# Blocked triangular solves on one NeuronCore: doubling-step products on half of the moving columns

## The chip, the core and the metric

The kernel runs on one core of a Trainium2 chip. TensorE multiplies a stationary operand (loaded into its array by a weight load) with a moving operand that streams through it, and writes to PSUM. VectorE (DVE) and ScalarE (ACT) do the elementwise work and copy results out of PSUM, SyncE (SP) issues the weight transfers from HBM, and GpSimd (POOL) does a little set-up. The engines run side by side and wait for each other with semaphores. The metric is the time of one execution on the device in microseconds (us). The median of three runs of the kernel before is 2916.0 us (2914.81 to 2918.55).

## What is computed

Two networks run one after the other on 256 tokens of width 1024: first two layers with feed-forward blocks and a four-way mixer (convolution, RWKV-7, retention, latent attention), then a pooling layer, a gated delta rule layer ("deltanet") and a mixture of experts. The change touches the two places where a recurrence is computed by chunks of 64 tokens. There a unit lower triangular 64x64 system is solved for each head and chunk:

```
a = jnp.einsum('bhnid,bhnjd->bhnij', k_beta, k) * decay
a = jnp.where(strict, a, 0.0) + jnp.eye(c, dtype=a.dtype)
u = lax.linalg.triangular_solve(a, v_beta, left_side=True, lower=True, unit_diagonal=True)
w = lax.linalg.triangular_solve(a, k_beta * jnp.exp(gc)[..., None],
                                left_side=True, lower=True, unit_diagonal=True)
```

In the reference the RWKV mixer is a scan over tokens, forward and backward. The kernel computes it by chunks too, so it has the same kind of system: a lower triangular one for the forward direction and an upper triangular one for the backward direction.

## The kernel before

Each engine has one program, written out by hand in a fixed order. Parts follow each other (`LAYER_PLAN` twice in a hardware loop, then `SECOND_PLAN`). Weights stream in 1 MB tiles through a ring of six buffers, `raw`; ScalarE rounds each tile to its high part (L282), VectorE makes the low part (L285), and TensorE multiplies with both. The RWKV part and the delta rule part (`rk_tensor`, `dn_core_tensor`) need few or no weights; their time is that of a long chain between TensorE and VectorE.

A triangular matrix is inverted by doubling. `T` holds the inverse of the diagonal blocks of a size, `TT` its transpose, `LT` the transpose of the off-diagonal matrix with its sign. The first doubling (blocks of 1 to 2) is made by VectorE before the solve. Five levels (`LEVELS`, `lv` 0 to 4) do the rest, blocks of 2, 4, 8, 16, 32:

- Y = L·T, then masked by VectorE to the off-diagonal block of each pair of blocks (L1131 on TensorE, L1151 on VectorE)
- T is increased by T·Y (L1140, added at L1157); the last level leaves this out
- TT is increased by the transpose of that product (L1144, added at L1161)

A solve has 16 matrices for each `d` (0 and 1), stacked as 8 groups of 64 columns by two halves of the 128 partitions (`HALVES`: partitions 0 to 63 and 64 to 127). So each product of a level is a group of 16 matmuls, 64 stationary columns by 64 moving columns, and the profile shows two records for an fp32 matmul: 32 records a group. The two halves use different rows and columns of the array. The names `rk_T`, `rk_TT`, `rk_Y`, `rk_LT` lie in the tensors `U` and `work`; those of the delta rule lie in `work`. `d` is the direction in the RWKV part and the token tile in the delta rule part. There are three solves: one in each of the two layers' RWKV part, and one in the delta rule.

Order of one level: TensorE does Y of d=0 and d=1, then an `extra` (at level 0 the RWKV part multiplies `rk_MK` by `rk_V`, L1328; at levels 0 to 3 the delta rule part transposes eight 128x128 tiles, L2037), then for each d T's product and TT's product. VectorE does the two masks, then T's and TT's sum for each d. TensorE waits for the mask of a `d` before T's product, and for T's sum before the next Y. After the RWKV solve TensorE goes on with L1406, and VectorE does L1564, the low part of a weight tile (L285) and the copies L1572, for which L1414 waits. After the delta rule's solve TensorE goes on with L2076.

Of the kernel before, what the change touches and what calls it, by code (L numbers as in the profile page):

```python
# [22 lines left out]
ALU = mybir.AluOpType  # L23
# [7 lines left out]
TT = S // P  # L31
# [143 lines left out]
def build(nc, a, out):  # L175

    with ExitStack() as ctx:
# [63 lines left out]
        f = {k: sem(k) for k in FLAGS + SOLVE_FLAGS}  # L241
# [868 lines left out]
        Y_BANK, ZT_BANK, ZTT_BANK = (0, 3), (1, 4), (2, 5)  # L1110
# [5 lines left out]
        def bank(i):  # L1116
            return ps[:, i, :].rearrange("p (g m) -> p g m", m=64)

        def eighths(r, i, g):
            return ps[r, i, g * 64:(g + 1) * 64]  # L1120

        def solve_tensor(pe, LT, T, TT, Y, first, extra):

            for lv in range(LEVELS):
                for d in range(2):
                    pe.wait_ge(f[f"sol_T{d}"], lv + 1)
                    if lv == 0:
                        first(d)
                    for g in range(8):
                        for r in HALVES:  # L1130
                            mm = pe.matmul(eighths(r, Y_BANK[d], g), LT[d][r, g, :], T[d][r, g, :], start=True, stop=True)  # L1131
                    mm.then_inc(f[f"sol_y{d}"], 1)
                extra(lv)
                for d in range(2):
                    pe.wait_ge(f[f"sol_ysb{d}"], lv + 1)
                    pe.wait_ge(f[f"sol_TT{d}"], lv + 1)
                    if lv < LEVELS - 1:
                        for g in range(8):
                            for r in HALVES:
                                mm = pe.matmul(eighths(r, ZT_BANK[d], g), TT[d][r, g, :], Y[d][r, g, :], start=True, stop=True)  # L1140
                        mm.then_inc(f[f"sol_z{d}"], 1)
                    for g in range(8):
                        for r in HALVES:
                            mm = pe.matmul(eighths(r, ZTT_BANK[d], g), Y[d][r, g, :], TT[d][r, g, :], start=True, stop=True)  # L1144
                    mm.then_inc(f[f"sol_z{d}"], 1)

        def solve_vector(dve, T, TT, Y, masks):
            for lv in range(LEVELS):
                for d in range(2):
                    dve.wait_ge(f[f"sol_y{d}"], lv + 1)  # L1150
                    dve.tensor_tensor(Y[d], bank(Y_BANK[d]), mask64(masks[d], lv + 1), ALU.mult) \  # L1151
                       .then_inc(f[f"sol_ysb{d}"], 1)
                dve.drain()
                for d in range(2):
                    if lv < LEVELS - 1:
                        dve.wait_ge(f[f"sol_z{d}"], 2 * lv + 1)
                        dve.tensor_tensor(T[d], T[d], bank(ZT_BANK[d]), ALU.add).then_inc(f[f"sol_T{d}"], 1)  # L1157
                        dve.wait_ge(f[f"sol_z{d}"], 2 * lv + 2)
                    else:
                        dve.wait_ge(f[f"sol_z{d}"], 2 * lv + 1)  # L1160
                    dve.tensor_tensor(TT[d], TT[d], bank(ZTT_BANK[d]), ALU.add).then_inc(f[f"sol_TT{d}"], 1)  # L1161
                dve.drain()

        CH = 64
# [31 lines left out]
        rk_B, rk_MK, rk_RK, rk_Kt, rk_T, rk_TT, rk_LT, rk_Y = ([carve_one() for _ in range(2)] for _ in range(8))  # L1196
# [14 lines left out]
        MASKS = (("low64", "up64", "strict_up64", "incl_up64"), ("up64", "low64", "strict_low64", "incl_low64"))  # L1211
# [120 lines left out]
        def eights(pair):  # L1332
            return [by_eight(v) for v in pair]
# [41 lines left out]
        def rk_tensor(pe, n, l):  # L1375
            pe.wait_ge(f["rk_kx"], 1)
            for b in range(2):
                mm = pe.matmul(half_of(2, b), const("bdones"), by_pair(rk_ksum)[:, b, :], start=True, stop=True)
# [11 lines left out]
            for b, c in BLOCKS:  # L1390
                for r in HALVES:
                    mm = pe.matmul(ps[r, 0, slot(b, c)], U[r, U_V + b, c * 64:(c + 1) * 64], eye64[r, :],
                                   start=True, stop=True)
# [2 lines left out]
            mix_out_tensor(pe, n, 2)  # L1396
            for d in range(2):
                rk_build_tensor(pe, d)
            solve_tensor(pe, eights(rk_LT), eights(rk_T), eights(rk_TT), eights(rk_Y), lambda d: rk_first_tensor(pe, d),
                         lambda lv: rk_x_tensor(pe) if lv == 0 else None)  # L1400
            for d in range(2):
                pe.wait_ge(f[f"sol_TT{d}"], LEVELS + 1)
# [139 lines left out]
        def rk_vector(dve, n, l):  # L1542
# [16 lines left out]
            for d in range(2):  # L1559
                refill_vector(dve, n + d + 1)  # L1560
                rk_evacuate_vector(dve, d)
            solve_vector(dve, eights(rk_T), eights(rk_TT), eights(rk_Y), (MASKS[0][0], MASKS[1][0]))
            for b in range(2):
                st = dve.scalar_tensor_tensor(out=by_pair(rk_prod)[:, b, :], in0=U[:, U_R + b, :],  # L1564
                                              scalar=layer_vec("rwkv_r_k")(b), in1=by_pair(rk_ksum)[:, b, :],
# [475 lines left out]
        def dn_core_tensor(pe):  # L2041
# [25 lines left out]
                if lv < 4:  # L2067
                    dn_turn_tensor(pe, 2 + lv, *((DN_V, 1), (DN_K, 1), (DN_Q, 0), (DN_Q, 1))[lv])

            solve_tensor(pe, dn_LT, dn_T, dn_TT, dn_Y, first, extra)  # L2070
            pe.wait_ge(f["dn_taken"], 6)
            for t in range(TT):
                pe.wait_ge(f[f"sol_TT{t}"], LEVELS + 1)
# [131 lines left out]
        def dn_core_vector(dve):  # L2205
# [16 lines left out]
            d_()  # L2222
            for t in range(TT):
                dve.tensor_tensor(dn_TT[t], dn_TT[t], bc(const("stack"), NH), ALU.add).then_inc(f[f"sol_TT{t}"], 1)
            solve_vector(dve, dn_T, dn_TT, dn_Y, ("low64", "low64"))
            for t in range(TT):
                dve.wait_ge(f["dn_u"], t + 1)
                dve.tensor_copy(dn_U[:, t], wide_two(2 + 2 * t)).then_inc(f["dn_us"], 1)
# [733 lines left out]
```

## Time and profile before

| | |
|---|---|
| median of three runs | 2916.0 us |
| profiled execution, its own time | 2916.18 us |
| its span | 2914.4 us |
| TensorE busy, share of the span | 93% |
| VectorE busy | 66% |
| ScalarE busy | 49% |
| mean granted TensorE clock | 0.969 of 2.4 GHz |
| first RWKV solve | 377.90 to 407.30 us |
| second RWKV solve | 1012.60 to 1042.10 us |
| delta rule solve | 1685.20 to 1720.10 us |

A busy share is an average over stages with different limits. The three solves take about 94 us of the 2914.4, so they are read by themselves: in the timeline, row by row, which engine starts as soon as which other has ended. A row of the timeline merges equal instructions: its start, its length from the first's start to the last's end, the engine, the line, the operation, and in brackets how long the engine sat idle before it and who released it. A matmul record's own length (219 ns here) is longer than the distance from one to the next, since they overlap; the rate is read from starts.

### The profile page before, as it was taken

The page shows a single profiled execution, that of the slowest core. Times are in us where ns is not written, and L with a number is a line of the kernel's source. Part 1 is how long each engine was busy: PE and PEld are TensorE (multiplying, and loading weights), DVE is VectorE, ACT ScalarE, POOL GpSimd, SP SyncE. Part 2 cuts the span into 40 slices and gives each one's busy share as a digit, 9 for nine tenths or more (in the row PEclk, how much of TensorE's full clock was granted, in tenths as well). Part 3 has the DMA queues.
Part 4 walks back from the last instruction along what each step waited for, and adds up shares of the span by engine and source line. Part 5 has one row for each costly group of instructions (what it writes and reads, how often), then busy time and mean ns, then how long its engine had stood idle before and what let it go on. Part 6 is the DMA issues. An engine that isn't in the chain of part 4 may idle for free.

```text
span 2914.4 us, 49969 instructions
## 1 busy us (share of the span) xinstructions
PE 2703.1 (93%) x20144; PEld 2382.9 (82%) x20144; DVE 1911.3 (66%) x1750; ACT 1419.3 (49%) x1330; POOL 84.6 (3%) x82
## 2 busy tenths in 40 slices
PE   8999989999999989986999896899999989999997
PEld 8988888989998879976999795687777777777876
DVE  4555765555555854555556645688878878888886
ACT  4343513343343513342336532566757666666665
POOL 6000005000000000000000000000000000000000
PEclk9999999999999999997999998899999999999999
DMA  7553213545553205542555400799989989999995
GB/s 274 181 191 130 93 46 130 187 159 174 187 189 107 94 17 184 187 156 87 187 187 146 145 3 8 283 338 344 344 292 340 342 296 336 337 342 336 341 346 197
DMA packets 340994, 602.08 MB, mean 207 GB/s; under 512 B 11968, under 2 KB 178752, under 8 KB 340672
## 3 DMA queue, kind: packets, MB, share of 16 engines
q1 hardware_dynamic: 333184, 590.84, 59.2%
q10 hardware_dynamic: 7616, 8.58, 0.9%
q8 instruction: 130, 2.13, 0.3%
q14 instruction: 64, 0.52, 0.1%
HBM read 598.34 MB, written 1.05 MB: 206 GB/s over the span
## 4 chain that ended last, share of the span: by engine, by line
DMA 54%; PE 22%; DVE 12%; ACT 8%; DVEq 2%; issue 1%; SPq 1%; another core or an unknown queue 0%; ACTq 0%; PEldq 0%; PEld 0%; POOLq 0%
DMA raw<-in_moe_w_up 26%; DMA raw<-in_ffn_w_down 22%; DVE wlo L285 8%; ACT whi L282 6%; PE ps L781 5%; PE ps L665 3%; DMA raw<-in_w_in 2%; PE ps L419 2%; PE ps L434 1%; PE ps L381 1%; DMA raw<-in_dn_w_out 1%; DMA raw<-in_dn_w_in 1%; DMA raw<-in_pool_w_in 1%; PE ps L1144 1%; PE ps L1131 1%
## 5 line engine op out<-in xcount | busy, mean ns | idle before, releaser
L285 DVE TENSOR_TENSOR wlo<-raw,whi 128x2048 fp32r<-128x2048 f32 x562 | 1286.4, 2289 | 623.1 <-ACT whi L282 621.7
L282 ACT CAST whi<-raw 128x2048 fp32r<-128x2048 f32 x562 | 1071.5, 1907 | 686.0 <-DMA raw<-in_ffn_w_down 171.5
L419 PE MATMUL ps<-xhi,whi 128*128 128x256 f32 x1760 | 500.4, 284 | 2.5 <-DVE xlo L369 2.5
L419 PE MATMUL ps<-xlo,whi 128*128 128x256 f32 x1760 | 498.7, 283 | 0.0
L419 PE MATMUL ps<-xhi,wlo 128*128 128x256 f32 x1760 | 498.7, 283 | 0.0
L2474 PE MATMUL ps<-whi,xhi 128*128 128x512 f32 x896 | 367.6, 410 | 21.3 <-remote 20.1
L2474 PE MATMUL ps<-whi,xlo 128*128 128x512 f32 x896 | 352.6, 394 | 0.0
L2474 PE MATMUL ps<-wlo,xhi 128*128 128x512 f32 x896 | 352.3, 393 | 0.0
L419 PEld LDWEIGHTS ps<-xhi,whi 128*128 128x128 f32 x1760 | 338.0, 192 | 5.2 <-DVE xlo L369 2.7
L419 PEld LDWEIGHTS ps<-xhi,wlo 128*128 128x128 f32 x1760 | 338.0, 192 | 1.9
L419 PEld LDWEIGHTS ps<-xlo,whi 128*128 128x128 f32 x1760 | 338.0, 192 | 0.0
L2474 PEld LDWEIGHTS ps<-whi,xhi 128*128 128x128 f32 x896 | 170.2, 190 | 62.2 <-issue 29.4
L2474 PEld LDWEIGHTS ps<-whi,xlo 128*128 128x128 f32 x896 | 169.8, 190 | 37.4
L2474 PEld LDWEIGHTS ps<-wlo,xhi 128*128 128x128 f32 x896 | 170.4, 190 | 36.2 <-issue 3.8
L2499 PE MATMUL ps<-whi,hhi 128*128 128x512 f32 x448 | 181.6, 405 | 15.5 <-DVE wlo L285 12.9
L434 PE MATMUL ps<-whi,hhi 128*128 128x512 f32 x472 | 185.7, 394 | 10.5 <-remote 7.2
L434 PE MATMUL ps<-wlo,hhi 128*128 128x512 f32 x472 | 184.5, 391 | 0.0
L434 PE MATMUL ps<-whi,hlo 128*128 128x512 f32 x472 | 183.9, 390 | 0.0
L2499 PE MATMUL ps<-whi,hlo 128*128 128x512 f32 x448 | 175.8, 392 | 0.0
L2499 PE MATMUL ps<-wlo,hhi 128*128 128x512 f32 x448 | 175.5, 392 | 0.0
L2499 PEld LDWEIGHTS ps<-whi,hhi 128*128 128x128 f32 x448 | 84.5, 189 | 54.6 <-issue 37.7
L487 ACT ACTIVATE work<-ps 128x512 f32<-128x512 f32 x55 | 32.9, 598 | 193.2 <-PE ps L419 193.2
(498 smaller groups left out, 3780.3 us busy)
## 6 DMA issues: line engine op xcount, KB each, us to landing
raw<-in_moe_w_gate SPq DMA_DIRECT2D x112, 1024.0 KB, 5.1
raw<-in_moe_w_up SPq DMA_DIRECT2D x112, 1024.0 KB, 5.1
raw<-in_moe_w_down SPq DMA_DIRECT2D x112, 1024.0 KB, 4.9
raw<-in_ffn_w_gate SPq DMA_DIRECT2D x55, 1024.0 KB, 5.0
raw<-in_ffn_w_up SPq DMA_DIRECT2D x55, 1024.0 KB, 5.0
raw<-in_ffn_w_down SPq DMA_DIRECT2D x55, 1024.0 KB, 4.8
raw<-in_w_in SPq DMA_DIRECT2D x26, 1024.0 KB, 5.0
raw<-in_dn_w_in SPq DMA_DIRECT2D x16, 1024.0 KB, 5.6
```

Source lines behind the costliest of these rows:

```text
L282: act.copy(whi[:, n % SPLIT, 0:width], raw[:, n % RAW, 0:width]).then_inc(hi_ready[n % SPLIT], 1)
L285: dve.tensor_tensor(wlo[:, n % SPLIT, 0:width], raw[:, n % RAW, 0:width], whi[:, n % SPLIT, 0:width], ALU.subtract).then_inc(split_ready[n ...
L381: mm = pe.matmul(turned_x(c, first)[:, t * P:(t + 1) * P], x[:, t, c * P:(c + 1) * P], turn[:, t, :], start=True, stop=True)
L419: mm = pe.matmul(dst[:, b * ntok:(b + 1) * ntok], w[:, n % SPLIT, c * GW + b * P:c * GW + (b + 1) * P], xt[part][:, c, 0:ntok], start=(c = ...
L434: mm = pe.matmul(ps[:, banks[2 * t + s], :], hp[part][b][:, t * P:(t + 1) * P], w[:, n % SPLIT, b * D + s * HALF:b * D + (s + 1) * HALF], ...
L487: act.activation(sil[:, q, 0:w], ps[:, 4 + q, 0:w], ACT.Silu)
L665: mm = pe.matmul(ps[0:m, bank, 0:S], wv, xt[:, c, :], start=first, stop=last)
L781: mm = pe.matmul(half_of(bank_, b, slice(0, m)), wv, xt[:, c, :], start=first, stop=last)
L1131: mm = pe.matmul(eighths(r, Y_BANK[d], g), LT[d][r, g, :], T[d][r, g, :], start=True, stop=True)
L1144: mm = pe.matmul(eighths(r, ZTT_BANK[d], g), Y[d][r, g, :], TT[d][r, g, :], start=True, stop=True)
L2474: mm = pe.matmul(dst, (xhi, xlo)[part][:, k * C // 2 + c, xhalf(q)], w[:, (m + k) % SPLIT, c * EW:(c + 1) * EW], start=(k == 0 and c == 0 ...
L2499: mm = pe.matmul(ps[:, s, :], (hh, hl)[part][:, g % 2, 2 * k + b, :], w[:, (m + k) % SPLIT, b * D + s * HALF:b * D + (s + 1) * HALF], star ...
```

## The change

The step of a level fills only half of the columns of T, and half of those of TT. For a lower triangular system these are, in T, the columns of the first block of each pair of blocks, and in TT those of the second; for an upper triangular one the other way round (`upper`, 0 or 1 for each d). The change multiplies and adds only these. Two helpers take the columns: at level `lv` the runs are `m = 2 << lv` columns long, every second run is taken, so 16 runs of 2 columns at level 0, 8 of 4, 4 of 8, 2 of 16, and at level 4 one run of 32.

The moving operand of all three products goes from 64 to 32 columns, and so does the output region in PSUM. The stationary operand stays 64 columns wide, the number of matmuls is the same, and so are all waits. The sums L1157 and L1161 go from 512 to 256 elements a partition. The mask L1151 still works on all 512 elements of Y, of which half are now what an earlier product left in that PSUM bank; the mask sets these to zero.

```diff
+        def half_cols(v, lv, other):
+
+            return v.rearrange("p (k a m) -> p k a m", a=2, m=2 << lv)[:, :, other, :]
+
+        def half_groups(v, lv, other):
+            return v.rearrange("p g (k a m) -> p (g k) a m", a=2, m=2 << lv)[:, :, other, :]
...
-                            mm = pe.matmul(eighths(r, Y_BANK[d], g), LT[d][r, g, :], T[d][r, g, :], start=True, stop=True)
+                            mm = pe.matmul(half_cols(eighths(r, Y_BANK[d], g), lv, upper[d]), LT[d][r, g, :],
+                                           half_cols(T[d][r, g, :], lv, upper[d]), start=True, stop=True)
...
-                                mm = pe.matmul(eighths(r, ZT_BANK[d], g), TT[d][r, g, :], Y[d][r, g, :], start=True, stop=True)
+                                mm = pe.matmul(half_cols(eighths(r, ZT_BANK[d], g), lv, upper[d]), TT[d][r, g, :],
+                                               half_cols(Y[d][r, g, :], lv, upper[d]), start=True, stop=True)
...
-                            mm = pe.matmul(eighths(r, ZTT_BANK[d], g), Y[d][r, g, :], TT[d][r, g, :], start=True, stop=True)
+                            mm = pe.matmul(half_cols(eighths(r, ZTT_BANK[d], g), lv, 1 - upper[d]), Y[d][r, g, :],
+                                           half_cols(TT[d][r, g, :], lv, 1 - upper[d]), start=True, stop=True)
...
-                        dve.tensor_tensor(T[d], T[d], bank(ZT_BANK[d]), ALU.add).then_inc(f[f"sol_T{d}"], 1)
+                        part = half_groups(T[d], lv, upper[d])
+                        dve.tensor_tensor(part, part, half_groups(bank(ZT_BANK[d]), lv, upper[d]), ALU.add) \
+                           .then_inc(f[f"sol_T{d}"], 1)
...
-                    dve.tensor_tensor(TT[d], TT[d], bank(ZTT_BANK[d]), ALU.add).then_inc(f[f"sol_TT{d}"], 1)
+                    part = half_groups(TT[d], lv, 1 - upper[d])
+                    dve.tensor_tensor(part, part, half_groups(bank(ZTT_BANK[d]), lv, 1 - upper[d]), ALU.add) \
+                       .then_inc(f[f"sol_TT{d}"], 1)
```

The instructions themselves show it. On TensorE, from the last matmuls of the build to level 1 of the RWKV solve, before (xN counts the matmuls of the program, two records each; the last figures are partitions x moving columns):

```order
L1313 MATMUL ps<-work 64x128 x16
L1131 MATMUL ps<-U 64x64 x32
L1328 MATMUL ps<-U,work 64x64 x32
L1140 MATMUL ps<-U 64x64 x16
L1144 MATMUL ps<-U 64x64 x16
L1140 MATMUL ps<-U 64x64 x16
L1144 MATMUL ps<-U 64x64 x16
L1131 MATMUL ps<-U 64x64 x32
L1140 MATMUL ps<-U 64x64 x16
```

and after, where lines are renumbered (L1138, L1148, L1153 are the three products, L1342 the extra):

```order
L1327 MATMUL ps<-work 64x128 x16
L1138 MATMUL ps<-U 64x16x2 x32
L1342 MATMUL ps<-U,work 64x64 x32
L1148 MATMUL ps<-U 64x16x2 x16
L1153 MATMUL ps<-U 64x16x2 x16
L1148 MATMUL ps<-U 64x16x2 x16
L1153 MATMUL ps<-U 64x16x2 x16
L1138 MATMUL ps<-U 64x8x4 x32
L1148 MATMUL ps<-U 64x8x4 x16
```

Nothing moved; the moving operand is 16 runs of 2 columns in place of 64 columns at level 0, and 8 runs of 4 at level 1.

On VectorE, from the sums of level 3 to the copies that stand behind the RWKV solve, before:

```order
L1157 TENSOR_TENSOR U<-U,ps 128x512
L1161 TENSOR_TENSOR U<-U,ps 128x512
L1151 TENSOR_TENSOR U<-ps,con 128x512 x2
L1161 TENSOR_TENSOR U<-U,ps 128x512 x2
L1564 SCALAR_TENSOR_TENSOR U<-U,cur 128x256 x2
L252 ISA
L285 TENSOR_TENSOR wlo<-raw,whi 128x2048
L1572 COPY work<-ps 128x256
```

and after (L1161 is now the mask, L1168 and L1174 are the sums, L1586 the copy):

```order
L1168 TENSOR_TENSOR U<-U,ps 128x16x16
L1174 TENSOR_TENSOR U<-U,ps 128x16x16
L1161 TENSOR_TENSOR U<-ps,con 128x512 x2
L1174 TENSOR_TENSOR U<-U,ps 128x8x32 x2
L1578 SCALAR_TENSOR_TENSOR U<-U,cur 128x256 x2
L252 ISA
L285 TENSOR_TENSOR wlo<-raw,whi 128x2048
L1586 COPY work<-ps 128x256
```

Again the order is the same. The sums have half the elements, the masks all of them.

## Rows read from the trace of the kernel before

**Rows 1.** Page, part 4: the chain that ended last, by line

```profile
DMA raw<-in_moe_w_up 26%; DMA raw<-in_ffn_w_down 22%; DVE wlo L285 8%; ACT whi L282 6%; PE ps L781 5%; PE ps L665 3%; DMA raw<-in_w_in 2%; PE ps L419 2%; PE ps L434 1%; PE ps L381 1%; DMA raw<-in_dn_w_out 1%; DMA raw<-in_dn_w_in 1%; DMA raw<-in_pool_w_in 1%; PE ps L1144 1%; PE ps L1131 1%
```

**Rows 2.** Stretches: us, busy (x records) of the engines, PEclk, DMA share, GB/s

```profile
377.90:407.30 29.40, 28.50 (x964) 28.40 (x960) 20.25 (x30) 1.21 (x3) 0.00 (x0) 1.00 0.08 27
...
1690.00:1693.00 3.00, 3.00 (x39) 2.67 (x39) 0.00 (x0) 1.60 (x7) 0.00 (x0) 0.50 0.00 0
...
1732.40:1736.00 3.60, 3.60 (x69) 3.60 (x65) 0.69 (x1) 1.01 (x1) 0.00 (x0) 1.00 0.02 5
```

**Rows 3.** Timeline, level 1 of the first RWKV solve: start, length, engine, line

```profile
386.45 2.06 PE L1131 MATMUL ps<-U 64*64 64x64 f32 x64
...
387.62 0.69 DVE L1151 TENSOR_TENSOR U<-ps,con 128x512 f32<-128x512 f32 x1 [0.24 <-PE ps L1131]
...
388.36 1.15 PE L1140 MATMUL ps<-U 64*64 64x64 f32 x32
...
389.35 1.10 PE L1144 MATMUL ps<-U 64*64 64x64 f32 x32
...
390.28 1.10 PE L1140 MATMUL ps<-U 64*64 64x64 f32 x32
...
391.21 1.10 PE L1144 MATMUL ps<-U 64*64 64x64 f32 x32
...
392.14 2.03 PE L1131 MATMUL ps<-U 64*64 64x64 f32 x64
```

**Rows 4.** Timeline, end of the first RWKV solve and what follows

```profile
403.50 2.03 PE L1131 MATMUL ps<-U 64*64 64x64 f32 x64
...
407.33 3.71 PE L1406 MATMUL ps<-work,U 64*64 64x128 f32 x64
407.52 0.69 DVE L1161 TENSOR_TENSOR U<-U,ps 128x512 f32<-128x512 f32 x1 [0.25 <-PE ps L1144]
408.31 0.88 DVE L1564 SCALAR_TENSOR_TENSOR U<-U,cur 128x256 f32<-128x256 f32 x2
409.11 2.28 DVE L285 TENSOR_TENSOR wlo<-raw,whi 128x2048 fp32r<-128x2048 f32 x1
...
411.53 0.42 DVE L1572 COPY work<-ps 128x256 f32<-128x256 f32 x1
...
412.34 0.33 PE L1414 MATMUL ps<-U,work 64*64 64x64 f32 x4 [1.30 <-DVE U L1572]
```

**Rows 5.** Timeline, end of the delta rule's solve

```profile
1719.33 0.69 DVE L1161 TENSOR_TENSOR work<-work,ps 128x512 f32<-128x512 f32 x1 [0.31 <-PE ps L1144]
1720.13 1.75 PEld L2076 LDWEIGHTS ps<-work 64*64 64x64 f32 x32
```

**Rows 6.** Groups by shape, VectorE: a sum with PSUM of 256 elements

```profile
L992 DVE TENSOR_TENSOR U<-ps,rope 32x256 f32<-32x256 f32 x2 | 0.8, 422 | 0.2
```

**Rows 7.** Timeline, weight loads of 128 columns for one moving column

```profile
1575.35 0.98 PEld L1847 LDWEIGHTS ps<-con,work 128*128 128x128 f32 x8
...
1576.25 0.19 PEld L665 LDWEIGHTS ps<-xhi,whi 128*128 128x128 f32 x1
```

**Rows 8.** Timeline, 128 stationary columns: 128 moving columns, then 64

```profile
1727.62 0.27 PE L2096 MATMUL ps<-U,work 64*128 64x128 f32 x1
...
1729.07 0.27 PE L2096 MATMUL ps<-U,work 64*128 64x128 f32 x1
...
1733.77 0.27 PE L2115 MATMUL ps<-rope,U 64*128 64x64 f32 x1
...
1735.78 0.27 PE L2117 MATMUL ps<-con,U 64*128 64x64 f32 x1
```

**Rows 9.** Timeline, delta rule's solve, level 0: two groups of 32 records

```profile
1691.30 1.98 PE L1140 MATMUL ps<-work 64*64 64x64 f32 x32
...
1693.06 1.17 PE L1144 MATMUL ps<-work 64*64 64x64 f32 x32
```

More of the change, by code:

```diff
@@ L1120, in eighths, with solve_tensor @@
             return ps[r, i, g * 64:(g + 1) * 64]
-        def solve_tensor(pe, LT, T, TT, Y, first, extra):
+        def half_cols(v, lv, other):
+            return v.rearrange("p (k a m) -> p k a m", a=2, m=2 << lv)[:, :, other, :]
+        def half_groups(v, lv, other):
+            return v.rearrange("p g (k a m) -> p (g k) a m", a=2, m=2 << lv)[:, :, other, :]
+        def solve_tensor(pe, LT, T, TT, Y, upper, first, extra):
             for lv in range(LEVELS):
@@ L1143, in solve_tensor, with solve_vector @@
                         for r in HALVES:
-                            mm = pe.matmul(eighths(r, ZTT_BANK[d], g), Y[d][r, g, :], TT[d][r, g, :], start=True, stop=True)
+                            mm = pe.matmul(half_cols(eighths(r, ZTT_BANK[d], g), lv, 1 - upper[d]), Y[d][r, g, :],
+                                           half_cols(TT[d][r, g, :], lv, 1 - upper[d]), start=True, stop=True)
                     mm.then_inc(f[f"sol_z{d}"], 1)
-        def solve_vector(dve, T, TT, Y, masks):
+        def solve_vector(dve, T, TT, Y, masks, upper):
             for lv in range(LEVELS):
@@ L1398, in rk_tensor @@
                 rk_build_tensor(pe, d)
-            solve_tensor(pe, eights(rk_LT), eights(rk_T), eights(rk_TT), eights(rk_Y), lambda d: rk_first_tensor(pe, d),
+            solve_tensor(pe, eights(rk_LT), eights(rk_T), eights(rk_TT), eights(rk_Y), (0, 1), lambda d: rk_first_tensor(pe, d),
                          lambda lv: rk_x_tensor(pe) if lv == 0 else None)
@@ L1561, in rk_vector @@
                 rk_evacuate_vector(dve, d)
-            solve_vector(dve, eights(rk_T), eights(rk_TT), eights(rk_Y), (MASKS[0][0], MASKS[1][0]))
+            solve_vector(dve, eights(rk_T), eights(rk_TT), eights(rk_Y), (MASKS[0][0], MASKS[1][0]), (0, 1))
             for b in range(2):
@@ L2068, in extra @@
                     dn_turn_tensor(pe, 2 + lv, *((DN_V, 1), (DN_K, 1), (DN_Q, 0), (DN_Q, 1))[lv])
-            solve_tensor(pe, dn_LT, dn_T, dn_TT, dn_Y, first, extra)
+            solve_tensor(pe, dn_LT, dn_T, dn_TT, dn_Y, (0, 0), first, extra)
             pe.wait_ge(f["dn_taken"], 6)
@@ L2224, in dn_core_vector @@
                 dve.tensor_tensor(dn_TT[t], dn_TT[t], bc(const("stack"), NH), ALU.add).then_inc(f[f"sol_TT{t}"], 1)
-            solve_vector(dve, dn_T, dn_TT, dn_Y, ("low64", "low64"))
+            solve_vector(dve, dn_T, dn_TT, dn_Y, ("low64", "low64"), (0, 0))
             for t in range(TT):
```

## The prediction

> **What bounds the kernel now.** I read the chain that ended last first. It shows what the whole kernel hangs on: weight transfers and the splitting of weights in most of its length, with the solve's matmuls at about 1% of the span for each of two lines [rows 1]. So most of the 2916 us is out of the change's reach, and the question is what the three solves do. The second view is the busy time by stretch. In the first solve TensorE is busy for 28.50 of 29.40 us, VectorE for 20.25, at a granted clock of 1.00, which is 2.4 GHz, while the transfers move 27 GB/s, next to nothing [rows 2]. No transfer runs there that could end last in place of the matmuls, so a microsecond saved in a solve should reach the end, and one lost too.
>
> The third view is the timeline of one level [rows 3]. Level 1 goes from 386.45 to 392.14, 5.69 us, and consists of six groups of 32 matmul records. From 389.35 to 390.28 and to 391.21 a group takes 0.93 us, so six take 5.6 and TensorE has only 0.1 us to wait in a level: the mask of d=0 starts 0.24 us after the last start of its group, takes 0.69, and by then the group of d=1 is nearly through (388.36). VectorE has nothing to do with the pace except there. The level is bound by how fast TensorE starts these small matmuls: 0.93/32 = 29.1 ns from record to record. The two partition halves run side by side, so one half starts a record every 58.2 ns.
>
> **What sets the 58 ns.** This is the step that decides. A record has two costs that overlap with those of its neighbours: the 64 moving columns and the load of the 64 stationary columns. The change halves the first and leaves the second. Which is longer can't be seen at 64 by 64, so I look for shapes where they differ.
>
> - Moving columns up, stationary the same: L1406 has 64 stationary and 128 moving columns. Its 64 records take 3.71 us, less the last one's own 0.27, over 63 steps 54.6 ns, 109 a half [rows 4]. Moving columns cost here, at (109.2 - 58.2)/64 = 0.80 ns each.
> - Stationary columns alone: L1847 loads 128 columns for a single moving column. Eight loads go from 1575.35 to 1576.25, 112.5 ns each [rows 7]. With one moving column there is nothing else to pay, so a load of 128 columns costs some 112 ns and one of 64 some 56.
> - Moving columns down, stationary the same, in two halves as in the solve: L2096 has 128 stationary and 128 moving columns, and its own half's 14 records start from 1727.62 to 1729.07, 111.5 ns apart. L2115, L2116, L2117 and L2120 have 128 stationary and 64 moving columns; their 37 records, which alternate between the halves, start from 1733.77 to 1735.78, 55.8 ns apart, so 111.7 for one half [rows 8]. Half of the moving columns, and the same pace.
>
> So the load sets a floor of about 0.87 ns a stationary column for each half, and 64 by 64 sits at the point where both costs are equal. Below 64 moving columns I expect the load to hold the 58 ns. The bounds: from above no change, 58.2 ns; from below half of L2115's 111.7, 55.9 ns a half or 27.9 a record, which would give 84 groups (28 a solve: six in levels 0 to 3, four in level 4) x 32 x 1.2 ns = 3.2 us. I take no change, because the last bullet has the same structure as the case, and there the pace with fewer moving columns did not go down by even 1 ns.
>
> **The change part by part.**
>
> - The three products on 32 columns: 84 groups, 0 us each, range 0 to -3.2 us in all.
> - T's and TT's sums on 256 elements: 0.689 falls to about 0.422 [rows 6], 0.27 us for each of 54. Within a level none is waited for: T's sum of d=0 has almost three groups (2.8 us) before the next Y needs it, and a sum or mask starts when TensorE releases it (all brackets in rows 3 and 4 say PE). If the short runs cost VectorE the whole 0.69 again, nothing changes there either.
> - Where a sum is waited for: behind the RWKV solve VectorE works without a break from the last sum at 407.52 through L1564 and L285 to the copy at 411.53, and TensorE's L1414 waits for those copies, 1.30 us [rows 4]. The last sum is released by TensorE, whose pace stays, and ends 0.27 us earlier, so L1414 starts 0.27 us earlier, in two layers: 0.54 us. Next late would be L1406's results, which are out at about 411.0, so they still cover nothing of it.
> - Behind the delta rule's solve the sum ends at 1720.02 and the next load starts at 1720.13, with its group done at about 1720.0 [rows 5]: 0.13 us to gain, then TensorE's own pace.
> - The mask L1151 is unchanged. No wait is added, nothing is queued behind something new, and no transfer moves.
>
> Sum: 0.54 + 0.13 = 0.7 us. The profiled execution took 2916.18 us (span 2914.4 and 1.8 around it), 0.2 above the median, so 2915.5 for it and **2915.3 us** by the median. About 0.2%, or 5.8 us, is what a measurement of this kernel can tell from no change.
>
> **Rivals.**
>
> - *The moving columns set the pace.* If a load of 64 columns were cheap or hidden in a way that one of 128 isn't, a group would take 0.93 us less 16 records of a half x 32 columns x 0.80 ns, 0.52 us. A level is then 0.52 + 0.24 + 0.69 + 0.05 until the first mask is in, 1.50, and four groups, 2.08: 3.58 in place of 5.69, 2.1 us less in four levels. In the last level, which has two groups behind the mask, the final sum now ends 408.21 - 403.50 = 4.71 us after the level's start [rows 4]; it would end at 1.50 + 1.04 + 0.24 + 0.42 = 3.20: 1.5 us. That is 9.9 us a solve, and some 29 us for three: 2887. For it: L1406 shows that columns cost above 64. Against it: rows 7 and 8.
> - *Part of that.* The load is a little shorter than I read, and the pace goes three tenths of the way from 29.1 ns a record to the 16.3 (0.52 us/32) of the rival above, to 25.3: 84 x 32 x 3.8 ns = 10 us, 2905. Rows 8 speak against it, by their 27.9. The Trainium skill, "TensorE: Matmul & The Clock Gate", in its section on the 56 ns gap, says that matmul starts never come closer than about 25 ns however few the columns. By that floor alone the gain would be 11 us, 2904, and the full gain of the first rival could not come. The trace has no spacing under 27.9 ns in the rows read, and does not show the floor itself.
> - *Short runs are slow, the time goes up.* At level 0 the moving operand and the output are 16 runs of 2 columns. No row read has such a pattern. It decides from the point where a column of such a run costs over about twice 0.80 ns, since until then 32 of them fit under the load. At four times, a group of level 0 would cost like one of 128 columns: 32 x 54.6 ns = 1.75 us, 0.82 more, six groups and three solves: 14.8 us, 2930. The Trainium skill, "Advanced Engine Details and Errata", section Memory Cachelines, says that a non-contiguous pattern in PSUM slows matmuls significantly, and also that every two consecutive elements should be contiguous for best throughput. By its first sentence it speaks against this change; by its second the runs of 2 are just long enough. No trace row bears on it.
> - *The clock falls, the time goes up.* The array's moving work in the solves is halved while its instructions keep their pace. Between 1690 and 1693 us, after TensorE had stood idle, the granted clock is 0.50 (1.2 GHz) [rows 2], and a group of the solve takes 1.76 us there, from 1691.30 to 1693.06 [rows 9], 0.83 more. Seven of the 84 groups at that clock are enough to be told; one whole solve would be 28 x 0.83 = 23 us, all three 70 us, 2939 to 2986. Against it: in the stretch of L2115 with its 64 moving columns under loads of 128 the clock is 1.00 [rows 2], and no wait gets longer; but it is a short stretch.
> - *It doesn't do what it says.* If the sums' patterns ran at the old 0.69, the 0.7 us goes: 2916.0, the same verdict.
>
> **How the numbers follow.** The forecast, pace unchanged: 0.75, which holds 2912 (the 3.2 us bound) to 2917. The moving columns set the pace: 0.09. Part of it: 0.06. Short runs slow: 0.05. The clock falls: 0.05. That gives faster 0.15, same 0.75, slower 0.10. The range runs from 2903 to 2924: it takes in the partial gain at 2905 and, above, a few microseconds of slower level-0 groups, and leaves out the full gain (0.09) and most of the two slower cases (0.10), 0.19 in all.
>
> **What the profile after would show.** If I am right, the timeline of level 1 has group starts 0.93 us apart with 32 moving columns, a level of about 5.7 us, weight loads at the same distance, VectorE sums of about 0.42 us with longer idle times before them, and a granted clock of 1.00 through the solve. L1414 starts 4.55 us after the start of the last sum, in place of 412.34 - 407.52 = 4.82. If the moving columns set the pace, the group starts are 0.5 apart and TensorE waits about half a microsecond for the first mask in each level. If runs of 2 are slow, level 0 alone has longer groups and level 4, with one run of 32, has none. If the clock falls, the stretches show it under 1.00 and the loads lengthen with the matmuls. I am wrong above all if a load of 64 columns is not half of one of 128.

## The result, and the profile after

The change makes the kernel slower. Its median is 2936.0 us (2929.7 to 2936.7, five runs), against 2916.2 us (2914.8 to 2918.6, five runs) for the kernel before on the same chip. The ratio is 1.0062, with a 95% interval of 1.0048 to 1.0077, so about 20 us or 0.6% are lost. The profiled execution took 2936.7 us, the longest of the five; its span is 2934.8.

The chain that ended last is built as before, with each of the solve's two lines still at 1%, [rows 1]:

```profile
DMA raw<-in_moe_w_up 26%; DMA raw<-in_ffn_w_down 22%; DVE wlo L285 7%; ACT whi L282 6%; PE ps L781 5%; PE ps L665 3%; DMA raw<-in_w_in 2%; PE ps L419 2%; PE ps L434 1%; PE ps L381 1%; PE ps L1153 1%; DMA raw<-in_dn_w_out 1%; PE ps L1138 1%; DMA raw<-in_dn_w_in 1%; DMA raw<-in_pool_w_in 1%
```

It doesn't show where 20 us went, so the two traces have to be laid side by side by stretch. In the changed kernel L2051 transposes the eight 128x128 tiles (L2037 before), L1138 is Y's product, L1148 and L1153 are T's and TT's products, L1161 is the mask and L1168 and L1174 are the sums.

**The RWKV solves are as forecast.** The timeline of level 1 of the first one (start, length, engine, line, shapes) answers to [rows 3]:

```profile
389.25 2.06 PE L1138 MATMUL ps<-U 64*64 64x32 f32 x64
...
393.06 1.10 PE L1148 MATMUL ps<-U 64*64 64x32 f32 x32
393.99 1.10 PE L1153 MATMUL ps<-U 64*64 64x32 f32 x32
...
395.14 0.42 DVE L1174 TENSOR_TENSOR U<-U,ps 128x256 f32<-128x256 f32 x1 [0.51 <-PE ps L1153]
```

The products now have 32 moving columns, their groups still start 0.93 us apart, and the sum takes 0.42 us with a longer wait ahead of it. The end of the same solve answers to [rows 4]:

```profile
410.00 3.69 PE L1420 MATMUL ps<-work,U 64*64 64x128 f32 x64
410.22 0.42 DVE L1174 TENSOR_TENSOR U<-U,ps 128x256 f32<-128x256 f32 x1 [0.51 <-PE ps L1153]
...
414.77 0.33 PE L1428 MATMUL ps<-U,work 64*64 64x64 f32 x4 [1.08 <-DVE U L1586]
```

From the last sum's start to the start of L1428 (L1414 of before) it is 414.77 - 410.22 = 4.55 us, the figure that was named, and the wait there is 1.08 us in place of 1.30.

**The delta rule's solve is where the time goes.** Its level 0 starts like that of before: Y's two groups, then a wait for ScalarE, of 2.34 us here and 2.31 before. TensorE's timeline from there on:

```profile
1692.53 1.36 PE L2051 MATMUL ps<-con,U 128*128 128x128 f32 x8 [2.34 <-ACT work L2190]
1693.82 1.92 PE L1148 MATMUL ps<-work 64*64 64x32 f32 x32
...
1700.66 3.60 PE L1138 MATMUL ps<-work 64*64 64x32 f32 x64
1704.20 1.97 PE L2051 MATMUL ps<-con,U 128*128 128x128 f32 x8
1706.10 1.92 PE L1148 MATMUL ps<-work 64*64 64x32 f32 x32
1707.82 1.90 PE L1153 MATMUL ps<-work 64*64 64x32 f32 x32
...
1712.94 3.60 PE L1138 MATMUL ps<-work 64*64 64x32 f32 x64
...
1744.33 3.64 PE L2090 MATMUL ps<-work 64*64 64x128 f32 x32
1747.78 1.94 PE L2095 MATMUL ps<-work 64*64 64x128 f32 x32
```

In the kernel before, one group takes 1.76 us behind this wait and the transposes, and the next is already short [rows 9]. Here every group up to 1744 takes 1.71 us (1706.10 to 1707.82 to 1709.53), and a level takes 12.28 us (1700.66 to 1712.94). The stretches give the reason (us, busy time and records of PE, PEld, DVE, ACT and POOL, the granted clock, DMA share, GB/s):

```profile
1690.00:1700.00 10.00, 7.66 (x132) 7.22 (x130) 3.53 (x7) 4.64 (x18) 0.00 (x0) 0.66 0.01 2
1700.00:1720.00 20.00, 20.00 (x320) 19.21 (x318) 4.87 (x9) 5.75 (x23) 0.00 (x0) 0.50 0.01 2
1720.00:1740.00 20.00, 20.00 (x350) 19.60 (x349) 5.30 (x11) 2.82 (x11) 0.00 (x0) 0.50 0.01 2
```

Stretches of 0.2 us place the edges: the granted clock is still 1.00 when TensorE resumes at 1692.53, falls to 0.50, 1.2 GHz, at about 1693.2 inside the transposes, and stays there to the end of the solve, although TensorE is busy in all of it. It comes back at about 1747.8, behind the first 32 records of L2090, which have 128 moving columns: they take 3.45 us and the next 32, L2095's, take 1.77. In the kernel before it fell too (at about 1689.8, with the transposes starting at 1689.57), but was back at about 1693.2, behind the transposes and one group of 64 columns:

```profile
1692.00:1694.00 2.00, 2.00 (x54) 2.00 (x54) 0.68 (x1) 1.57 (x7) 0.00 (x0) 0.70 0.00 0
1694.00:1720.00 26.00, 26.00 (x801) 25.30 (x796) 16.53 (x25) 8.58 (x32) 0.00 (x0) 1.00 0.02 4
```

The balance of the two spans, by TensorE's starts of the same steps: the solve begins 3.0 us later (1685.18 and 1688.13). Nearly all of that stands ahead of any changed instruction: the first RWKV solve begins at 377.90 before and at 380.75 after, but at 376.66 in half_filled below, whose code up to there is the changed kernel's, so it is a spread between executions. The solve takes 35.0 us before and 56.2 after, **21.2 us more**. Up to the routing of the experts another 1.6 us are lost, in L2090's first records. From the routing to the end it is 1103.7 us before and 1098.3 after, 5.4 less. Together 3.0 + 21.2 + 1.6 - 5.4 = 20.4, the difference of the spans.

### The profile page after: what moved, and what is told of

It is laid out like the page before. It is cut to its first block, busy times and chain, and to the rows that moved or that the text cites. A ratio compares the mean times of both kernels' runs of the same rounds, so it can differ in the third digit from the quotient of the medians.

```text
span 2934.8 us, 49951 instructions
## 1 busy us (share of the span) xinstructions
PE 2723.4 (93%) x20126; PEld 2404.3 (82%) x20144; DVE 1897.3 (65%) x1750; ACT 1419.7 (48%) x1330; POOL 81.1 (3%) x82
## 4 chain that ended last, share of the span: by engine, by line
DMA 53%; PE 23%; DVE 12%; ACT 7%; DVEq 2%; issue 1%; SPq 1%; another core or an unknown queue 0%; ACTq 0%; PEldq 0%; PEld 0%; POOLq 0%
DMA raw<-in_moe_w_up 26%; DMA raw<-in_ffn_w_down 22%; DVE wlo L285 7%; ACT whi L282 6%; PE ps L781 5%; PE ps L665 3%; DMA raw<-in_w_in 2%; PE ps L419 2%; PE ps L434 1%; PE ps L381 1%; PE ps L1153 1%; DMA raw<-in_dn_w_out 1%; PE ps L1138 1%; DMA raw<-in_dn_w_in 1%; DMA raw<-in_pool_w_in 1%
## 5 line engine op out<-in xcount | busy, mean ns | idle before, releaser
L2488 PEld LDWEIGHTS ps<-whi,xhi 128*128 128x128 f32 x896 | 169.4, 189 | 60.5 <-issue 28.3
```

The source lines that it names most:

```text
L2488: mm = pe.matmul(dst, (xhi, xlo)[part][:, k * C // 2 + c, xhalf(q)], w[:, (m + k) % SPLIT, c * EW:(c + 1) * EW], start=(k == 0 and c == 0 ...
```

## The experiments

The theory: groups of 32 moving columns hold a clock of 2.4 GHz that they find, but don't bring one of 1.2 GHz back. Its rivals: the strided columns themselves are slow, in this solve or in some level of it; the shorter sums disturb something; or the loss is not in the solve at all. Each edit below is shown against the changed kernel. `cols_y` stands for the choice of Y's columns and `cols_z` for that of T's and TT's; both give either the 32 columns of `half_cols` or all 64.

**One solve or the other.** In rk_half the two RWKV solves have the change and the delta rule's has not; in dn_half it is the reverse.

```diff
+            rk = upper == (0, 1)
+            def cols_y(v, lv, other):
+                return half_cols(v, lv, other) if rk else v
...
-            mm = pe.matmul(half_cols(eighths(r, Y_BANK[d], g), lv, upper[d]), LT[d][r, g, :],
-                           half_cols(T[d][r, g, :], lv, upper[d]), start=True, stop=True)
+            mm = pe.matmul(cols_y(eighths(r, Y_BANK[d], g), lv, upper[d]), LT[d][r, g, :],
+                           cols_y(T[d][r, g, :], lv, upper[d]), start=True, stop=True)
```

> The change in the two RWKV solves alone; the delta rule's solve is as before. Theory A (the 20 us are the delta rule's solve, where TensorE's clock falls to 1.2 GHz in a 2.3 us wait and does not come back while the groups have 32 moving columns): no loss here, 2915.5 us (ratio 1.000, at most 0.5 us gained from the shorter last sums), granted clock in the delta rule's solve back at 1.00 from about 1693 us on. Rival B (the loss has to do with short runs or half columns in all three solves): two thirds of it, 2929 us.

Measured: 2917.5 us against 2915.4, ratio 1.0008 (0.9998 to 1.0017). Two thirds of the changed groups cost nothing. The delta rule's solve has 64 columns again, and after its wait of 2.32 us the clock is back inside L1160's group, the second one of 64 columns, which takes 1.41 us to the next start at 1695.74:

```profile
1692.57 1.98 PE L1155 MATMUL ps<-work 64*64 64x64 f32 x32
1694.33 1.57 PE L1160 MATMUL ps<-work 64*64 64x64 f32 x32
```

> The change in the delta rule's solve alone. Theory A: the whole loss, 2936 us (ratio 1.006 to 1.007), granted clock 0.50 from the wait at level 0 to the end of the solve, groups 1.7 us apart. Rival B: a third of it, 2923 us. Rival C (the clock fell by chance of its phase in that kernel and not by the columns): the clock is back at 1.00 in some of the runs, times spread between 2914 and 2936.

Measured: 2936.6 us, ratio 1.0077 (1.0060 to 1.0093): the whole loss. Its four executions lie between 2935.3 and 2938.5, so the spread down to 2914 that rival C of the expectation asks for isn't there. The clock in its stretch of 50 us:

```profile
1695.00:1745.00 50.00, 50.00 (x834) 48.81 (x834) 12.69 (x25) 8.60 (x32) 0.00 (x0) 0.50 0.01 2
```

The last level's groups lie in that stretch too. Their 32 columns are one run, without a stride, and in the changed kernel they take 3.42 and 3.41 us for 64 records (starts 1737.50, 1740.92, 1744.33), 1.71 a group like the others. So it isn't the strides that keep the clock down.

**The sums alone.** In sums_half all products have 64 columns (`half_cols` only where the condition is `False`), and the sums stay at half of the columns.

> VectorE's sums on half of the columns in all three solves, TensorE's products on all 64 columns. Theory A: the clock comes back as before, and the 0.7 us of the prediction's sum are left: 2915.3 us (ratio 0.9998). Rival D (the shorter sums change when TensorE's work comes, and that keeps the clock down): 2936 us.

Measured: 2914.7 us, ratio 0.9997 (0.9987 to 1.0006). The sums are out, as a loss and as a gain that can be told.

**Level 0 alone.** dn_level0_full gives the delta rule's level 0 its 64 columns back (`half_cols(...) if rk or lv > 0 else v`); levels 1 to 4 keep 32.

> The change everywhere but in the products of level 0 of the delta rule's solve, which have all 64 columns. Theory A, in its form that 32 columns hold a clock of 2.4 GHz but don't raise one of 1.2: the clock rises in level 0 at about 1693 us as before and stays, groups of levels 1 to 4 are 0.93 us apart: 2915.5 us. Rival E (in the delta rule's solve 32 columns can't hold the clock either, since the transposes and waits between thin out the work): the clock rises in level 0 and falls again in level 1 or 2: 2930 us or more.

Measured: 2914.7 us, ratio 0.9998 (0.9988 to 1.0007). Four fifths of the solve have the changed form, and none of the loss is there:

```profile
1689.26 1.17 PE L1160 MATMUL ps<-work 64*64 64x64 f32 x32
...
1695.10 1.12 PE L1155 MATMUL ps<-work 64*64 64x32 f32 x32
1696.05 1.10 PE L1160 MATMUL ps<-work 64*64 64x32 f32 x32
```

The groups of level 1, with 32 columns, are 0.95 us apart here and 1.72 in the changed kernel (1706.10 to 1707.82). Same instructions, same strides, same level; what differs is the clock that they found. Taken alone, this run leaves open that level 0's runs of two columns are slow by themselves. The RWKV solves, whose level 0 has the same runs, speak against it, and half_filled below settles it: there this very level 0 has them 0.95 us apart.

**Y alone at 64 columns.** In dn_y_full the delta rule's Y products have 64 columns and T's and TT's have 32, at all levels.

> In the delta rule's solve the first product of each level (Y) has all 64 moving columns, the two others 32; RWKV solves as in the change. Theory A: the clock can't rise at level 0 behind the wait, where the four groups have 32 columns, and may rise in the two groups of 64 at the start of a later level: between 2915.5 (at once in level 1: 2919) and 2936 us (never). The kernel shows whether two groups of 64 among four of 32 are enough.

Measured: 2917.9 us, ratio 1.0004 (0.9994 to 1.0014).

```profile
1696.34 1.90 PE L1160 MATMUL ps<-work 64*64 64x32 f32 x32
1698.05 2.94 PE L1145 MATMUL ps<-work 64*64 64x64 f32 x64
...
1701.94 1.12 PE L1155 MATMUL ps<-work 64*64 64x32 f32 x32
```

The four groups of 32 columns of level 0 run at half pace, as in the changed kernel. Then come Y's 64 records with 64 columns, and within them the clock returns: they take 2.87 us to the next start, where at 2.4 GHz it is 2.0 (1705.69 to 1707.69 here) and at 1.2 GHz 3.5. The 32-column groups behind them run at full pace. So one pair of groups of 64 columns does what four groups of 32 didn't, and in the changed kernel 26 didn't.

**The wait filled.** If the wait of 2.3 us is what costs the clock, then matmuls into it should keep it. half_filled is the changed kernel with eleven matmuls of zeros, bf16, 512 moving columns, into a PSUM bank that is free there:

```diff
             def extra(lv):
+                if lv == 0:
+                    for _ in range(11):
+                        pe.matmul(ps[:, 2, :], zero[:, 0:P], zero[:, :], start=True, stop=True)
```

full_filled has the same fill with all products at 64 columns, that is the kernel before with shorter sums and the fill.

> The changed kernel with 11 more matmuls (bf16 zeros, 128x512, into a PSUM bank that is free then) in the delta rule's solve at level 0, in the wait of TensorE for ScalarE before its transposes. Their results are used by nothing. Theory A: TensorE is not idle, the clock stays at 1.00, and 32 columns hold it through the solve: 2913 to 2914 us (the 20 us back, and the 1.6 us that the kernel before loses at half clock between 1690 and 1693). If 32 columns lose the clock by themselves, it falls later in the solve: 2925 us or more.

> The same 11 matmuls in the wait, products on all 64 columns, sums on half. Theory A: as half_filled, 2913 to 2914 us (ratio 0.999), since the pace of a group does not depend on whether it has 32 or 64 moving columns. It is the candidate that could beat both kernels; a gain of 2 us is at the edge of what can be measured.

Measured: 2911.1 us for half_filled, ratio 0.9984 (0.9974 to 0.9993), and 2908.1 us for full_filled, ratio 0.9973 (0.9964 to 0.9982), against 2916.0 for the kernel before. Both are faster than either kernel. The timeline of half_filled:

```profile
1685.47 2.55 PE L2083 MATMUL ps<-zero 128*128 128x512 bf16 x11
1687.88 1.09 PE L2051 MATMUL ps<-con,U 128*128 128x128 f32 x8
1688.91 1.12 PE L1148 MATMUL ps<-work 64*64 64x32 f32 x32
1689.86 1.10 PE L1153 MATMUL ps<-work 64*64 64x32 f32 x32
```

The fill lasts as long as the wait did, L2051 follows without idle time, and all 32-column groups are at full pace: the solve takes 33.2 us, against 56.2 without the fill. In full_filled it takes 33.3, against 35.0 before. This is the strongest of the runs: the solve's own instructions are those of the change, not one altered, and its 21 us are gone. Whether full_filled is the better of the two is open: the means of their executions are 2.8 us apart (2910.3 of ten, 2907.5 of eleven), each with a spread of some 2.8, and nothing in the two traces accounts for it. Its gain of 7.8 us is more than its solve accounts for (1.7 us); that is taken up below.

**The same loss made elsewhere.** The RWKV solves find a clock of 2.4 GHz. If that is all that protects them, a wait ahead of them should put them at 1.2. idle_half repeats a VectorE product that TensorE then waits for, ahead of each RWKV solve; idle_full does so with all products at 64 columns.

```diff
+            pe.wait_ge(f["rk_eMK"], 2)
             if d:
-                pe.wait_ge(f["rk_eMK"], 2)
                 pe.wait_ge(f["rk_etok"], 2)
...
+            for _ in range(6 * d):
+                dve.tensor_tensor(by_eight(rk_RK[d]), banks_two(3, 1), mask64(incl), ALU.mult)
+                dve.drain()
```

> The changed kernel with a wait put before each RWKV solve: VectorE repeats one of its operations six times (same result) and TensorE waits for it, idle for some 5 us. Theory A: the clock falls to 0.50 in the wait and does not come back in the solve with 32 moving columns: each of the two solves gets 20 to 24 us longer than with the same wait and 64 columns, 2936 + 8 (the wait) + 40 to 48 = 2984 to 2992 us. Rival F (only the delta rule's solve has that trouble, by its transposes or its place): the clock comes back within about 4 us, some 2948 us.

> The same wait before each RWKV solve, products on all 64 columns, sums on half. Theory A: the clock falls in the wait and is back at 1.00 within a few groups: 2915 + 8 (the wait) + 2 x 2 to 3 us = 2927 to 2930 us. Rival F expects about the same here.

Measured: 2952.6 us for idle_half, ratio 1.0131 (1.0115 to 1.0146), and 2926.7 for idle_full, ratio 1.0038 (1.0025 to 1.0051). The second is about as expected, the first is a **miss** by over 30 us. Its timeline says why:

```profile
383.32 3.62 PE L1138 MATMUL ps<-U 64*64 64x32 f32 x64 [6.31 <-DVE work L1532]
386.73 3.68 PE L1342 MATMUL ps<-U,work 64*64 64x64 f32 x64
390.18 1.76 PE L1148 MATMUL ps<-U 64*64 64x32 f32 x32
391.75 1.12 PE L1153 MATMUL ps<-U 64*64 64x32 f32 x32
```

The wait of 6.31 us did cost the clock, and Y's groups of 32 columns didn't bring it back. But level 0 of an RWKV solve issues another product between Y's groups and the rest, L1342, which has 64 moving columns and is no part of the change. It runs at half pace to its end, and the clock is back shortly behind it: at about 391.6, inside the group L1148, and in the second layer at about 1036.8, at that group's end. So the clock rose while a group of 32 columns ran, and this run alone doesn't say that it was L1342's doing. The next pair bears it out: there such groups follow each other without that product, and the clock stays down. The expectation had counted the solve's own groups only.

**The wait behind that product.** late_half and late_full put the wait where no product of 64 columns follows: the mask of level 0, d=0, is repeated nine times, so that TensorE waits inside the solve, behind the extra product (L1345 in late_half, the same product under the numbering of that kernel).

```diff
+                    for _ in range(9 if upper == (0, 1) and lv == 0 and d == 0 else 0):
+                        dve.tensor_tensor(Y[d], bank(Y_BANK[d]), mask64(masks[d], lv + 1), ALU.mult)
+                        dve.drain()
```

> The changed kernel with a wait inside each RWKV solve, at level 0 behind the extra product with its 64 moving columns: VectorE repeats the first mask nine times (same result) and TensorE waits some 4 us for it. From there to the end of the solve all groups have 32 moving columns. Theory A (32 columns hold 2.4 GHz but don't raise the clock from 1.2): the clock falls in the wait and stays at 0.50 for the 26 groups behind it; each of the two solves is some 20 us longer than in late_full, so 2936 + 2 x (4 + 20) = 2984 us. Rival G (the RWKV solves differ from the delta rule's in something else than the extra product, so that 32 columns do raise the clock there): back at 1.00 within about 4 us, 2950 us.

> The same wait in the RWKV solves, products on all 64 columns, sums on half. Theory A: the clock falls in the wait and is back within some 3 us, as in the delta rule's solve of the kernel before: 2915 + 2 x (4 + 1.5) = 2926 us. Rival G expects the same here; the difference to late_half decides.

Measured: 2988.7 us for late_half, ratio 1.0250 (1.0233 to 1.0267), and 2928.7 for late_full, ratio 1.0039 (1.0025 to 1.0053), both near what was expected, though in late_full the clock took 5.6 us to return (388.57 to 394.2), not the 3 of the expectation. In late_half, as timeline and as stretches:

```profile
387.12 1.92 PE L1148 MATMUL ps<-U 64*64 64x32 f32 x32 [4.27 <-DVE U L1164]
...
431.52 4.75 PE L1423 MATMUL ps<-work,U 64*64 64x128 f32 x64
```

```profile
387.00:400.00 13.00, 12.88 (x242) 12.88 (x244) 4.15 (x9) 0.00 (x0) 0.00 (x0) 0.50 0.01 3
400.00:430.00 30.00, 30.00 (x568) 30.00 (x567) 8.78 (x17) 0.00 (x0) 0.00 (x0) 0.50 0.01 2
```

And in late_full, with the same wait and 64 columns:

```profile
400.00:430.00 30.00, 28.90 (x857) 28.26 (x853) 17.54 (x31) 1.29 (x4) 0.00 (x0) 1.00 0.12 39
```

An RWKV solve, harmless in the change, now shows the delta rule's picture: 44 us at 0.50 with 32 columns, the clock back only in L1423 with its 128. With 64 columns it was back at about 394.2, inside the fourth group behind the wait, where the delta rule's solve of the kernel before had needed one group. The two kernels differ by 60.0 us; less the 21.2 that dn_half lost to the delta rule, 38.8 are left for two solves, 19.4 each. The loss moves with the wait, not with the solve.

**The pace by itself.** The forecast rested on weight loads that set the pace. In pace, series of 64 products of different shapes stand ahead of L1343 in the first RWKV solve, as in this one:

```diff
+            for rep in range(2):
+                for b, c in BLOCKS:
+                    for r in HALVES:
+                        pe.matmul(ps[r.start:r.start + 32, 1, slot(b, c)][:, 0:32], S[r, b, c, 0:32], M[r, b, c, 0:32],
+                                  start=True, stop=True)
```

> The changed kernel with seven series of 32 more matmuls at level 0 of each RWKV solve, into a PSUM bank that is free then; nothing uses their results. Stationary x moving columns: 64x64, 64x32, 64x16, 64x32 in runs of one column, 32x64, 32x32, 32x16. If the load of the stationary columns is the floor, as the prediction argued: 64x32, 64x16 and the runs of one column go at the 29 ns a record of 64x64; 32x32 and 32x16 go at about half, 15 to 16 ns a record, unless another floor is above that (the Trainium skill's page TensorE: Matmul & The Clock Gate gives about 25 ns from start to start); 32x64 at 29 ns, by its moving columns. If short runs cost more, the runs of one column are slower than 64x32.

Measured (a single execution, 2959.6 us, with seven such series in each RWKV solve). The first layer:

```profile
379.63 2.09 PE L1352 MATMUL ps<-U 64*64 64x64 f32 x64
381.53 2.04 PE L1356 MATMUL ps<-U 64*64 64x32 f32 x64
383.37 2.13 PE L1360 MATMUL ps<-U 64*64 64x16 f32 x64
385.27 3.66 PE L1364 MATMUL ps<-U 64*64 64x32 f32 x64
388.87 3.46 PE L1369 MATMUL ps<-U 64*32 64x64 f32 x64
392.17 1.17 PE L1374 MATMUL ps<-U 64*32 64x32 f32 x64
393.18 1.16 PE L1379 MATMUL ps<-U 64*32 64x16 f32 x64
```

```profile
385.30:388.80 3.50, 3.50 (x69) 3.50 (x66) 0.00 (x0) 0.00 (x0) 0.00 (x0) 0.50 0.02 5
388.90:392.10 3.20, 3.20 (x63) 3.20 (x64) 0.00 (x0) 0.00 (x0) 0.00 (x0) 0.51 0.00 0
392.20:393.10 0.90, 0.90 (x66) 0.90 (x62) 0.00 (x0) 0.00 (x0) 0.00 (x0) 1.00 0.00 0
```

From start to start over 64 records, at 2.4 GHz: with 64 stationary columns 29.7 ns a record for 64 moving columns, 28.8 for 32 and 29.7 for 16. With 32 stationary columns 15.8 ns for 32 moving ones and 17.0 for 16. The two series between them ran at 1.2 GHz in this layer. The second layer has all seven at a granted clock of 1.00:

```profile
1032.99 2.05 PE L1360 MATMUL ps<-U 64*64 64x16 f32 x64
1034.86 2.06 PE L1364 MATMUL ps<-U 64*64 64x32 f32 x64
1036.85 1.98 PE L1369 MATMUL ps<-U 64*32 64x64 f32 x64
1038.66 1.18 PE L1374 MATMUL ps<-U 64*32 64x32 f32 x64
```

L1364 takes every second column, runs of one, and needs 31.1 ns a record, 2.3 more than L1356's 28.8. L1369, 32 stationary columns with 64 moving ones, needs 28.3. So with 64 stationary columns the load sets the floor; a shorter load does what fewer moving columns don't, but only where the moving columns are few as well.

The clock differs between the layers. In the first it fell at about 385.2, at the end of the series with 16 moving columns and without idle time; L1364 with 32 ran at half pace to its end, and at the end of L1369, with its 64 moving columns, it came back. In the second it never fell, with the same instructions in the same order. What made the difference isn't shown.

## Why the prediction was wrong

It said 2915.3 us, range 2903 to 2924, no change at 0.75. It is 2936.0, slower. Step by step:

- *What bounds the kernel; a microsecond lost in a solve reaches the end.* Right in the main: 21.2 us lost in the solve came out as 20 in all. The exception is the 5.4 us less behind the routing.
- *The load sets 58 ns a half.* Right. 0.93 us a group, 5.65 a level in the RWKV solves, and the pace run measures the floor with the moving columns varied by a factor of four; its 28.3 ns for 32 stationary and 64 moving columns bears out that the two costs are about equal at 64 by 64. The rival in which the moving columns set the pace, and the partial one, fell: at 64 stationary columns no series goes below 28.8 ns.
- *The sums: 0.42 us, L1414 earlier by 0.27.* Right, 4.55 us behind the last sum's start. The 0.54 us can't be told in the time, as was said.
- *Short runs.* They cost nothing under the load, in runs of 2 to 32 (RWKV solves at 0.93 us a group throughout, rk_half 1.0008). The sentence of the Trainium skill, "Advanced Engine Details and Errata", section Memory Cachelines, by which a non-contiguous pattern slows matmuls significantly is not borne out here for such runs; only runs of one cost something, 31.1 against 28.8 ns a record in pace.
- *Three products on 32 columns: 84 groups, 0 us each, 0 to -3.2.* **This term failed.** It took the clock of 1.00 of [rows 2]'s first stretch for all 84 groups. But the second stretch of [rows 2] and both rows of [rows 9] show that the delta rule's 28 meet a clock of 1.2 GHz in their level 0. For those the cost of a group hangs on a second question: who brings the clock back. In the kernel before it was the first 64-column groups; the change took just that away. The right price could have been formed from [rows 9], whose 1.76 us a group at 1.2 GHz is near the 1.71 that came out. With the measured figures: 28 groups x (1.71 - 0.93) = 21.8 us; less Y's two groups of level 0, which still find 2.4 GHz (1.6), and less what the kernel before lost on its own two groups behind the wait (0.9); plus 0.87 for each set of L2051's transposes at levels 1 to 3 (2.6), less 0.4 on level 0's, which is shorter here: 21.5, measured 21.2.
- *The clock rival, 0.05.* The mechanism's name and its price were right: one whole solve, 23 us, 2939. What failed was its case. I asked only whether less moving work makes the clock **fall**, and answered with L2115 at 64 moving columns, which found the clock at 1.00 and kept it. That shows holding. Whether it lets the clock **rise** again was never asked, though the place where it has to rise was in the rows. The forecast's "no wait gets longer" was true and beside the point: the wait that was already there was enough. Asked rightly, the rival had one definite solve, one definite moment and one price, and should have had a large part of the chance. As for the range, it ended at 2924 although this rival's only whole case began at 2939.

**What stays open.** The time from the routing to the end is 1103.7 us in the kernel before and 1103.8 in sums_half, but 1098.3 in the changed kernel, 1096.0 in half_filled, 1095.9 in full_filled and 1096.1 in idle_half, with 1101.1 in rk_half and 1101.0 in dn_level0_full between them. The number of columns in the solves doesn't sort these figures, so the 5.4 us aren't shown to be an effect of the change. A part of it stands in the first 50 us behind the routing. Here before:

```profile
1810.70:1860.70 50.00, 31.76 (x136) 26.85 (x137) 26.47 (x68) 15.97 (x13) 0.00 (x0) 0.74 0.53 190
```

and here after:

```profile
1836.50:1886.50 50.00, 31.69 (x145) 26.43 (x147) 28.61 (x70) 17.54 (x14) 0.00 (x0) 0.79 0.57 207
```

The transfers move 17 GB/s more there, 0.85 MB, which at the 326 to 340 GB/s of the stretches behind it is about 2.6 us. Why, isn't settled: the code is the same, and the kernels in which the time is shorter include slower ones and faster ones. The profiled executions of half_filled and full_filled were also 5.7 and 4.9 us under the medians of their kernels, so their stretches can't be set against the medians. So of full_filled's 7.8 us only 1.7 are explained, by the transposes and the group behind the wait that now run at 2.4 GHz; the rest was measured and not explained. Open too is what exactly the chip wants to see before it grants 2.4 GHz. The runs show which groups did it and which didn't, not a rule.

## What to carry to other kernels

Before you thin out matmuls, look at the granted clock at which each stretch of them begins, and ask of every stretch that begins at half of full speed which instruction brings the clock back and whether the change weakens it; that it holds elsewhere is no answer. Moving columns below the stationary ones buy no time, since the weight load goes on at its own pace (28.8 to 29.7 ns a record here, whether there were 64, 32 or 16); only fewer stationary and fewer moving columns together did. And a short wait of TensorE ahead of a run of small matmuls is worth filling with matmuls of zeros: here it took 1.7 us off a solve with 64 columns and 23.0 off one with 32.

## What the runs showed of the hardware

- **Holding the clock and regaining it are different things.** Groups of 64 stationary and 32 moving columns, two halves side by side, kept 2.4 GHz through levels 1 to 4 of an RWKV solve (389 to 410 us, of a solve of 29 us at 1.00 throughout) and, in half_filled, through 27.8 us of the delta rule's, and stayed at 1.2 GHz for 50 us in dn_half and for 43 us in late_half, with TensorE busy in 99 to 100% of those stretches. The busy share didn't tell the two apart. The eight 128x128 transposes in each of the delta rule's levels 0 to 3 (L2051, 1.90 us at that clock) didn't help either. The clock came back inside or shortly behind 64 records with 64 moving columns (Y's in dn_y_full, L1342's in idle_half) and 32 to 64 with 128 (L2090, L1423); in late_full it took until the fourth group of 64 columns.
- **The clock can fall without any idle time:** at the end of L1360's series, 16 moving columns over 64 stationary ones, in the first layer of pace (0.50 from 385.2 us on). In the second layer the same series kept 1.00, so it is one case of two in a single execution.
- **Behind a wait of 2.3 us the clock was at half**, in each kernel that leaves TensorE idle there (1.00 until 0.2 to 0.7 us after TensorE resumed, in the seven traces that have it), and with matmuls of zeros in its place it stayed at 1.00.
- **Records of two partition halves start closer together than 25 ns.** With 32 stationary and 32 moving columns it is 15.8 ns from record to record, 31.6 for one half. The Trainium skill, "TensorE: Matmul & The Clock Gate", in its section on the 56 ns gap, says that matmul starts never come closer than about 25 ns; for records that alternate between two halves the measurement decides otherwise, and for a single half it shows nothing below.
